# Reordering one head's vector, GpSimd and load sequence in a hybrid mLSTM and latent-attention step

## What is computed

```python
# per head, d = 512; prompt: zero state; streams: carried state C, n, m
s = einsum('bhtd,bhsd->bhts', q, k) * w_intra
num = w_inter * einsum('bhvk,bhtk->bhtv', C, q) + einsum('bhts,bhsv->bhtv', s, v)
den = w_inter * einsum('bhk,bhtk->bht', n, q) + sum(s, -1)
h = num / maximum(abs(den), exp(-m_t))
C_new = decay * C + einsum('bhsv,bhsk->bhvk', v * w_upd, k)
n_new = decay * n + einsum('bhs,bhsk->bhk', w_upd, k)
# after the scan, per token and head
hn = (h - mean(h)) * rsqrt(var(h) + EPS) * outnorm_w
y = (hn + skip * xc) * silu(z)          # the sample skip and the gate product
x = x + y @ w_out
```

## Time and profile before

| | us |
|---|---|
| median of 3 runs | 1041.86 |
| lowest, highest | 1040.7, 1042.16 |
| the profiled execution | 1039.92 |
| its span | 1038.1 |
| PE busy in the span | 1010.7 |
| DVE busy | 520.0 |
| POOL busy | 300.6 |

### The profile page before, as it was taken

The page is one execution under the profiler, slowest core; times in us unless marked ns, Lnnn a source line. Parts: engine busy times, 40 slices in busy tenths (PEclk is TensorE's granted clock), DMA queues, the critical chain, the costliest instruction groups (busy, mean ns, idle before and its releaser), DMA issues.

```text
span 1038.1 us, 12026 instructions
## 1 busy us (share of the span) xinstructions
PE 1010.7 (97%) x4310; PEld 648.1 (62%) x4310; DVE 520.0 (50%) x1149; ACT 258.0 (25%) x541; POOL 300.6 (29%) x361
## 2 busy tenths in 40 slices
PE   7999999999989999999999999999999999999998
PEld 5777777777754453443535677777766666656655
DVE  6955444444466566685665522334244444344224
ACT  3212121212154242232421000011213323243221
POOL 3652525252313234142232053411440303010110
PEclk9999999999999999999999999999999999999999
DMA  7324232423275988979799432022210201213202
GB/s 271 98 80 158 97 113 105 157 91 111 112 286 191 399 329 345 370 303 392 300 350 340 154 107 71 32 81 104 93 63 1 84 17 68 73 47 128 79 27 102
DMA packets 44465, 164.21 MB, mean 158 GB/s; under 512 B 4916, under 2 KB 8248, under 8 KB 35456
## 3 DMA queue, kind: packets, MB, share of 16 engines
q1 hardware_dynamic: 44416, 163.56, 42.8%
HBM read 106.32 MB, written 57.23 MB: 158 GB/s over the span
## 4 chain that ended last, share of the span: by engine, by line
PE 85%; DVE 8%; ACT 2%; POOL 2%; DMA 1%; issue 1%; SPq 0%; DVEq 0%; POOLq 0%; ACTq 0%
PE work_a L825 11%; PE work_b L825 9%; PE work_a L720 7%; PE work_b L720 5%; PE work_b L1258 5%; PE work_a L1049 5%; PE bank L1133 5%; PE work_b L1342 4%; PE work_a L948 4%; PE bank L770 3%; PE bank L1016 2%; PE work_b L1133 2%; PE work_b L1001 2%; DVE arena L2181 2%; PE work_a L1328 2%; PE bank L1303 2%
## 5 line engine op out<-in xcount | busy, mean ns | idle before, releaser
L2181 DVE SCALAR_TENSOR_TENSOR arena<-arena,bank 128x512 f32<-128x512 f32 x128 | 87.1, 743 | 58.7 <-PE bank L1016 58.7
L1049 PE MATMUL work_a<-arena 128*128 128x512 f32 x128 | 64.1, 613 | 2.8 <-ACT arena L1611 2.8
L825 PE MATMUL work_a<-arena 128*128 128x320 f32 x224 | 64.9, 433 | 0.4 <-DVE arena L1948 0.4
L825 PE MATMUL work_a<-arena,ring 128*128 128x320 f32 x224 | 64.9, 432 | 0.0
L825 PE MATMUL work_b<-arena 128*128 128x320 f32 x224 | 62.8, 432 | 0.0
L720 PE MATMUL work_a<-arena,ring 128*128 128x320 f32 x192 | 54.2, 441 | 6.8 <-DMA ring<-in_stream 6.8
L825 PEld LDWEIGHTS work_b<-arena 128*128 128x128 f32 x224 | 42.6, 190 | 17.7
L720 PE MATMUL work_b<-arena,ring 128*128 128x320 f32 x192 | 52.8, 432 | 0.0
L2716 POOL COPY arena<-arena 32x640 f32<-32x640 f32 x20 | 16.9, 844 | 123.1 <-ACT arena L1726 116.9
L825 PEld LDWEIGHTS work_a<-arena 128*128 128x128 f32 x224 | 41.5, 190 | 16.1 <-issue 0.6
L825 PEld LDWEIGHTS work_a<-arena,ring 128*128 128x128 f32 x224 | 41.5, 190 | 15.5
(11 more groups left out here) (349 smaller groups left out, 1917.4 us busy)
## 6 DMA issues: line engine op xcount, KB each, us to landing
ring<-in_stream SPq DMA_DIRECT2D x66, 512.0 KB, 3.7
arena<-in_c SPq DMA_DIRECT2D x32, 1024.0 KB, 9.2
out_s_c<-arena SPq DMA_DIRECT2D x32, 1024.0 KB, 6.6
arena<-in_keys SPq DMA_DIRECT2D x8, 664.0 KB, 4.1
v_scratch<-arena SPq DMA_DIRECT2D x16, 320.0 KB, 4.4
k_scratch<-arena SPq DMA_DIRECT2D x16, 320.0 KB, 4.7
z_scratch<-arena SPq DMA_DIRECT2D x16, 320.0 KB, 4.2
arena<-k_scratch SPq DMA_DIRECT2D x4, 1280.0 KB, 12.6
```

The costliest lines, as they stand in the source:

```text
L825: last = mm(quarter[q], weights[:, k, :], tokens_of[:, k, :], start=fresh and k == 0, stop=k == KH - 1, skip_group_check=True)
L1049: last = mm(pair_bank[q % 2], kh[:, q, t, :], vh[:, :, t, :], start=t == 0, stop=t == NP - 1)
L2181: op = v.scalar_tensor_tensor(ct[s % CS][:, g, :], ct[s % CS][:, g, :], decb[:, h, b:b + 1], bank[g][:, :], ALU.mult, ALU.add)
```

## The change

Three edits in stage B. On DVE the statistics of tiles 2 and 3 come ahead of the sample skip of the head before. On POOL the inverse roots of tiles 2 and 3 and the second `add_k` come ahead of the gate product of the head before's sample tile. On SP the load of z goes from a head's second step to its fourth, behind `load_c` and ahead of the store of part 0.

```diff
@@ SP, stage_b
-                    if n == 1:
+                    if n == 3:
                         if h:
                             sp.wait_ge(y_ready, 2 * h)
                         sp.dma_start(zh, chunks(z_dram, h, slice(0, T))).then_inc(hz_in, 16)
@@ DVE
                 update(h, 1)
+                statistics(h, 2)
+                statistics(h, 3)
                 if h:
                     add_skip(h - 1, slice(SEQ, T), NP)
-                statistics(h, 2)
-                statistics(h, 3)
                 update(h, 2)
@@ POOL
                 inverse_root(h, 0)
                 inverse_root(h, 1)
+                add_k(h, 1)
+                inverse_root(h, 2)
+                inverse_root(h, 3)
+                add_k(h, 2)
                 if h:
                     gated(h - 1, slice(SEQ, T), 2)
-                add_k(h, 1)
-                inverse_root(h, 2)
-                add_k(h, 2)
-                inverse_root(h, 3)
                 add_k(h, 3)
```

## The result

| | before | changed |
|---|---|---|
| median, us | 1042.2 (6 runs) | 1053.88 (6 runs) |
| lowest, highest | 1040.7, 1044.2 | 1050.05, 1058.19 |
| profiled execution | 1039.92 | 1055.44 |
| its span | 1038.1 | 1053.7 |
| mean granted clock of the runs | 1.000 in the profiled one | 0.986 to 0.992 |

The ratio is 1.011 with a 95% interval of 1.0082 to 1.0138. The direction was forecast, the size was not: 1047.9 was predicted, with 1052.5 as the upper end.

The account below looks back on a forecast made before the run. PE, busy nearly throughout, was taken as the bound, at a head's end by the landing of part 1's store. Net +1.5 us a head, front's gain included, gave 4 × 1.5 = +6.0 on 1041.86: 1047.9, range 1042.2 to 1052.5.

Parts of the forecast that it names:

- The front: Start of heads 1 to 3: PE's wait for tile 2's normalising is gone, −0.92 us each, −2.8 in all.
- The skip caught by POOL: Rival, heads 1 to 3: an `add_k` gets between the skip's instructions, at most 1.26 us more each, 1051.7; 10 in 100.
- The landing: End of each head: z's bytes delay the landing of part 1's store, which PE awaits; +1.5 us, between 0.55 and 2.3.
- The lower end, 0.55: Head 1's end: if a fuller queue keeps 422 GB/s, part 1's store lands only 0.55 us later.
- The sum: Whole kernel: 4 × 1.5 = +6.0 us, between 2.0 and 9.2, so a median of 1047.9.
- The free z load: Rival, heads' ends: z's bytes do not delay part 1's store, PE gains 0.92 us in heads 1 to 3, 1039.1; 8 in 100.
- the partly absorbed one: Rival, heads' ends: the landing moves by only 0 to 0.5 us a head, about 1042.9; 12 in 100.
- The front's wait: Rival, start of heads 1 to 3: something else releases tile 2 late, so the wait stays, 1050.7; 5 in 100.
- What would show it: Signs in the changed profile, among them ACT's second wait for `out_p_c` exceeding 6.3 us, else the queue reading is wrong.

Follow-up runs that it names:

- experiment 4: Changed kernel plus matmuls whose results nobody reads, five ahead of the last part's copy, four ahead of the output product: 1049.75 us, ratio to before 1.0074.
- experiment 1: Kernel before with only the z load moved from a head's second step to its fourth: 1053.56 us, ratio 1.0092.
- experiment 6: Kernel before with z loaded in two halves, one in the second step and one in the fourth: 1043.63 us, ratio 1.0013.
- experiment 2: Kernel before with only DVE's and POOL's lists changed, the z load staying in the second step: 1052.49 us, ratio 1.0112.
- experiment 9: Changed kernel with the z load moved from the fourth step to right behind part 1's store: 1048.15 us, ratio to before 1.0044.
- experiment 8: Changed kernel with part 1's store in step 4 and the z load in the third step: 1038.37 us, ratio to before 0.9976.

## Why the prediction was right on the waits and wrong on the time

**The front.** Right: −2.8 us, tile 2 no longer waited for, the two stretched instructions short.

**The skip caught by POOL.** It didn't happen. The skip took its 1.13 us beside the root. Update 2 began at 406.08, its first quarter (0.68 us) was done at 406.8, and the turn that asks for it came at 407.18: the margin was 0.4 us, where 0.3 had been worked out. Nothing waited at L1034.

**The landing.** Right in direction and in the mean; that the waits came to 6.1 us where 6.0 stood in the sum is partly luck. Taken: +1.5 us a head, between 0.5 and 2.3. Measured from PE's idle times, less the 0.92 us that PE came earlier in heads 1 to 3: head 0 2.88 − 1.28 = 1.6; head 1 3.19 − 0.31 − 0.92 = 2.0; head 2 3.32 − 1.55 − 0.92 = 0.9; head 3 2.62 − 0.92, less almost nothing before, 1.7. Together 6.1. So head 1, the one worked out, came near the upper end, and head 2 made up for it: there the store took 10.4 us to land before already, not 9.4, so head 2 did not "go the same way". In the changed kernel it took 12.0, 12.3, 12.4 and 11.5 us in heads 0 to 3, about the "11 to 12" of the prediction. The lower end, 0.55, rested on a rate of 422 GB/s and on 4.72 MB in 12.55 us. Neither holds. From the issue of step 3's store to the landing of part 1's it was 16.4 us in the kernel before, and 19.3 in the changed one:

```profile
411.50:427.90 16.40, 16.40 (x88) 6.85 (x86) 8.46 (x15) 3.09 (x9) 1.36 (x1) 1.00 1.00 374
```

```profile
414.34:433.64 19.30, 16.88 (x88) 6.85 (x86) 10.86 (x19) 3.09 (x9) 4.26 (x1) 1.00 1.01 384
```

That is 6.1 and 7.4 MB: z's 1.3 MB came on top whole, at a rate that hardly rose.

**The sum.** This is the step that failed. It priced each microsecond of waiting at one microsecond of time, and the range's upper end did too. PE's waits at the heads' ends grew from at most 1.6 us to 2.6 to 3.3 us, and behind each the clock ran at its lower level for 3.4 or 6.8 us. In the profiled execution that is a further term of 9.3 us, beside 6.1 us of waits; from the changed kernel's median to that of experiment 4 it is 4.1. The prediction had worked out waits of 2 to 3.5 us and put what they do to the clock at nothing, without a reason. The rows of the kernel before had no price for it: their clock is 1.00 throughout and their longest wait there 1.6 us.

**The rivals.** The free z load and the partly absorbed one are out (experiments 1 and 6: all of z costs 9.5 us of waits by itself). The front's wait did not stay.

**What would show it.** ACT's wait for the part's store was to be longer than 6.3 us: it was 6.44 in head 1 but 5.06, 4.70 and 6.00 in heads 0, 2 and 3, since ACT's copy of part 2 comes later too (the store of part 0 lands late as well). As a test it was badly chosen; PE's wait is the right one.

## What to carry to other kernels

A wait on TensorE can have two prices: its own length, and the work behind it at half clock. Here none of the waits up to 1.6 us at the heads' ends had the second price and most of those from 2.6 us on did, so 6.1 us of longer waits became 11.7 us of time. Where one queue feeds everything, look for the small store that gates a buffer and issue it ahead of the bulk: moving one 256 KB store up by a few places took away every wait that this change had lengthened. When an engine's list is changed, look at the place of the DMA that it releases: with the new orders alone, z's old place held up SP's whole list. And a wait that is taken away can uncover a shorter one behind it, as at L900, where half of the gain went.

## What the runs showed of the hardware

At the ends of the heads the clock fell behind every PE idle time of 3.0 to 4.0 us (seven in the profiles of the changed kernel and of experiments 1 and 2), behind 2.62 and 2.88 us in the changed kernel, not behind 2.75 (experiment 2) and 2.84 us (experiment 1), and never behind 1.6 us or less. In experiment 9 it fell in a wait of 4.09 us within a projection. It can fall while PE still waits (0.7 us before its end in heads 1 and 2 of the changed kernel). The stretches lasted 3.4 or 6.8 us. The length of one wait doesn't tell the whole: the stretches at the start of stage B came with no idle time over 0.8 us in the 9 us before.

The changed kernel's executions scatter more (1050.05 to 1058.19) than those of the kernel before (1040.7 to 1044.2) and those with the waits filled (1049.35 to 1050.31, four executions). That the waits do this isn't shown: experiment 8, whose profile has none of them, spreads from 1035.35 to 1043.62.

A DVE instruction with two SBUF inputs that started 0.2 us behind the start of a POOL instruction of 4.50 us ended 0.3 us behind its end: 0.42 us became 4.58. One that started 0.8 or 1.2 us ahead of POOL's took 0.42.
